# Prompt attention: the shifts of a head turned to rows by one transpose instead of four

## The reference, cut to what matters

```
s_s = einsum(q_r, k_s) * scale ; p_s = masked_softmax(s_s, m_s) ; o_s = p_s @ v_s
s_w = einsum(q_r, k_w) * scale ; p_w = masked_softmax(s_w, m_w) ; o_w = p_w @ v_w
o   = g[0] * o_c + g[1] * o_s + g[2] * o_w        # o_c: the compressed branch
```

## Time and profile before

| | us |
|---|---|
| time, median of 3 runs (1668.59 to 1669.82) | 1668.79 |
| span of the profiled execution, first to last instruction | 1663.0 |
| PE busy, share of the span | 97% |
| DVE busy | 50% |
| ACT busy | 39% |
| POOL busy | 7% |
| q_row copies (L1891), 16 of them, busy in all | 10.9 |
| transposes of the shifts (L1695), 64 of them, busy in all | 10.0 |

### The profile page before, as it was taken

The page is one execution under the profiler, slowest core; times in us unless marked ns, Lnnn a source line. Parts: engine busy times, 40 slices in busy tenths (PEclk is TensorE's granted clock), DMA queues, the critical chain, the costliest instruction groups (busy, mean ns, idle before and its releaser), DMA issues.

```text
span 1663.0 us, 32232 instructions
## 1 busy us (share of the span) xinstructions
PE 1605.1 (97%) x13788; PEld 1472.4 (89%) x13788; DVE 824.2 (50%) x1091; ACT 648.4 (39%) x1141; POOL 117.2 (7%) x146
## 2 busy tenths in 40 slices
PE   8999899999999999999999779999999999999998
PEld 7787699999999999999999545556999999999998
DVE  6988547434343346633343465652473433434372
ACT  5444655323131334521232366665442222323242
POOL 1000000000000000010240352210000000000000
PEclk9999999999999999999999989999999999999999
DMA  7633161332323222322146200002223232322221
GB/s 204 160 93 113 35 206 56 104 98 77 102 77 100 78 82 71 102 83 77 53 135 211 92 1 1 1 14 77 76 77 102 76 102 77 102 77 87 92 77 54
DMA packets 139623, 145.69 MB, mean 88 GB/s; under 512 B 6562, under 2 KB 131314, under 8 KB 139279
## 3 DMA queue, kind: packets, MB, share of 16 engines
q1 hardware_dynamic: 138207, 136.94, 26.2%
q0 software_dynamic: 1280, 6.75, 1.3%
HBM read 130.79 MB, written 10.87 MB: 85 GB/s over the span
## 4 chain that ended last, share of the span: by engine, by line
PE 86%; DVE 7%; ACT 4%; issue 2%; DMA 0%; SPq 0%; DVEq 0%; ACTq 0%
PE ps L389 62%; PE ps L522 2%; PE ps L1215 2%; PE ps L1064 2%; PE ps L1063 2%; PE ps L1065 2%; PE ps L1737 2%; PE ps L1717 2%; DVE w_lo L374 1%; PE ps L1719 1%; PE ps L1664 1%; PE ps L575 1%; ACT w_hi L369 1%; PE ps L1662 1%; DVE resid L688 1%
## 5 line engine op out<-in xcount | busy, mean ns | idle before, releaser
L389 PE MATMUL ps<-x_hi,w_hi 128*128 128x272 f32 x1664 | 360.8, 290 | 11.5 <-DVE x_lo L2530 4.3
L389 PE MATMUL ps<-x_hi,w_lo 128*128 128x272 f32 x1664 | 357.8, 289 | 0.0
L389 PE MATMUL ps<-x_lo,w_hi 128*128 128x272 f32 x1664 | 356.6, 288 | 0.0
L374 DVE TENSOR_TENSOR w_lo<-w_raw,w_hi 128x2048 fp32r<-128x2048 f32 x101 | 233.8, 2315 | 141.4 <-ACT w_hi L369 139.5
L369 ACT ACTIVATE w_hi<-w_raw 128x2048 fp32r<-128x2048 f32 x101 | 192.6, 1907 | 267.6 <-PE ps L389 264.9
L389 PEld LDWEIGHTS ps<-x_hi,w_hi 128*128 128x128 f32 x1664 | 266.9, 189 | 20.5 <-issue 11.5
L389 PE MATMUL ps<-hid_hi,w_hi 128*128 128x272 f32 x1280 | 268.0, 289 | 2.2 <-DVE hid_lo L2038 1.5
L389 PE MATMUL ps<-hid_hi,w_lo 128*128 128x272 f32 x1280 | 267.4, 288 | 0.0
L389 PEld LDWEIGHTS ps<-x_lo,w_hi 128*128 128x128 f32 x1664 | 267.1, 189 | 0.0
L389 PE MATMUL ps<-hid_lo,w_hi 128*128 128x272 f32 x1280 | 266.6, 288 | 0.0
L389 PEld LDWEIGHTS ps<-x_hi,w_lo 128*128 128x128 f32 x1664 | 265.4, 189 | 0.0
(11 more groups left out here) (378 smaller groups left out, 2140.9 us busy)
## 6 DMA issues: line engine op xcount, KB each, us to landing
w_raw<-in_ffn_w_in SPq DMA_DIRECT2D x64, 512.0 KB, 4.5
w_raw<-in_ffn_w_out SPq DMA_DIRECT2D x64, 512.0 KB, 4.3
w_raw<-in_nsa_w_in SPq DMA_DIRECT2D x20, 512.0 KB, 4.5
w_raw<-in_ple_w_gate SPq DMA_DIRECT2D x16, 512.0 KB, 4.3
w_raw<-in_conv_w_in SPq DMA_DIRECT2D x15, 512.0 KB, 5.4
w_raw<-in_conv_w_out SPq DMA_DIRECT2D x8, 512.0 KB, 4.0
w_raw<-in_nsa_w_o SPq DMA_DIRECT2D x8, 512.0 KB, 4.5
conv_in_turned<-conv_in SPq DMA_DIRECT2D x16, 203.2 KB, 2.9
```

The lines of the kernel that those rows point to most:

```text
L374: dve.tensor_tensor(WL[par][:, :], RAW[par][:, :], WH[par][:, :].bitcast(F32), ALU.subtract)\
L389: m = pe.matmul(o_, w[par][:, wcols:wcols + P], x[:, k, c_], start=f, stop=l)
```

## The change

The tile `shift_hi_lo` grows from 32 to 228 columns and is cleared once, by a new memset ahead of L1336. The four shifts of query tile qt now stand at columns 32 qt to 32 qt + 3 of a head's part (the parts of even and odd heads start 128 columns apart; between the groups of four lie zeros). One transpose of 100 columns turns them; query tile qt's four rows come out in PSUM partitions 32 qt to 32 qt + 3, columns 0 to 127. Four copies of 4x128 bring them to where one copy of 4x512 did. The semaphore for the reader rises with the last of the four.

```diff
+        M_W = 3 * 32 + 4 + 4
+
+        def shift_cols(hd):
+
+            x = MROW[:, (hd % 2) * P:(hd % 2) * P + M_W - 4]
+            return x, bass.AP(x.tensor, x.offset, [x.ap[0], [32, QT], [2, 2], [1, 2]])
+
...
-                                               ("shift_hi_lo", [P, 2, QT, 2, 2], F32R), ("soft_cmp", [P, 3, QT, GQ], F32),
+                                               ("shift_hi_lo", [P, P + M_W], F32R), ("soft_cmp", [P, 3, QT, GQ], F32),
...
+            L(dve.memset(MROW[:, :].bitcast(F32), 0.0), wait=False)
             for br in range(2):
                 L(dve.tensor_tensor(SELC[HD:P, br:br + 1], CST[HD:P, C_ID + HD + 2 * br:C_ID + HD + 2 * br + 1],
...
-                for qt in range(QT):
-                    m = pe.transpose(PS[0:4, 7, qt * P:(qt + 1) * P],
-                                     MROW[:, hd % 2, qt, :, :].rearrange("p b h -> p (b h)").bitcast(F32), ID)
-                m.then_inc(S["m_T"], 1)
+                pe.transpose(PS[0:M_W - 4, 7, 0:P], shift_cols(hd)[0].bitcast(F32), ID).then_inc(S["m_T"], 1)
...
-                x, m = hd % 4, MROW[:, hd % 2, :, :, :]
+                x, m = hd % 4, shift_cols(hd)[1]
...
-                L(dve.tensor_copy(QB[c % 3][HD:HD + 4, half, :], PS[0:4, 7, :]), S["m_rows"], wait=False)
+                for qt in range(QT):
+                    L(dve.tensor_copy(QB[c % 3][HD:HD + 4, half, qt * P:(qt + 1) * P], PS[32 * qt:32 * qt + 4, 7, 0:P]),
+                      S["m_rows"] if qt == QT - 1 else None, wait=False)
```

## The result

The changed kernel takes 1675.08 us (median of 21 runs), the kernel before 1668.59 in as many runs of the same chips. The ratio is 1.0042, 95% interval 1.0029 to 1.0054: slower, 0.4% and not the 0.16% of the forecast, and outside its range. The runs of either kernel spread over 8 to 12 us (1661.95 to 1670.37, 1666.87 to 1678.74), far more than the three runs shown before. One slip in the text ahead: the new tile has 232 columns, not 228; its memset took 252 ns.

What follows compares the result with a forecast made beforehand. The prediction took PE (86% of the chain) and DVE (7%) as the bound. Its terms, 0.53 + 0.32 + 3.18 + 0.53 - 0.05 + 0.2 - 1.98 = +2.73 us, on 1668.79 gave 1671.5 us, range 1666.3 to 1673.6.

Steps and rivals of the forecast that it cites:

- an even head: PE at six even heads: one transpose in place of four on the chain saves 0.33 us each, 1.98 in all.
- serial copies: DVE's four copies of a head's rows don't overlap: 1.21 us against 0.68, +0.53; 3.18 over six odd heads.
- The memset: DVE ahead of L1336, on the chain: the larger clear adds +0.2 us, between 0 and 0.3.
- the line on the even heads: Even heads other than 0 and 8: copies end 0.20 us later against PE, DVE has pauses; costed at nothing.
- POOL works hard ahead of the steps: POOL busy 4.7 of 5 us there stretches copies inside SBUF but not the 4x512 copies from PSUM; costed at nothing.
- head 8: Copy on the chain, with a weight split and the maxima behind it on DVE: +0.53 us.
- head 15: Transposes on the chain, copy not: the turned matmul starts slightly earlier, -0.05 us.
- head 0: Ahead of the steps, where DVE is the bound: its longer copies on the chain cost +0.53 us.
- head 1: Ahead of the steps: copy starts 0.21 us earlier after the single transpose, then costs +0.53; net +0.32 us.
- overlapping copies: Rival on DVE's four copies: full overlap gives 1666.4 us, 0.08 us of overlap 1668.3; chance 0.22 together.
- a dear transpose: Rival on PE: the lone transpose costs 0.27 us, saves only 0.17; sum +3.7, 1672.5 us; chance 0.15.
- the clock's fall in the steps: Rival: PE's 1.17 us idle before odd heads' turned matmuls lowers its clock, 2.5 us on top, 1674 us; chance 0.05.

Runs made afterwards that it cites:

- the two-input form: Changed kernel with the compressed branch's minimum as a tensor_tensor against a constant column, not a tensor_scalar: ratio 1.0023, steps 1 to 47 165.41 us.
- the keys in two halves: Changed kernel with DVE doing the first half of a group's keys one step earlier: ratio 1.0037, steps 1 to 47 164.49 us.
- again: The changed kernel once more with no edit, against the kernel before: ratio 1.0028, steps 1 to 47 166.85 us.
- copies first: Changed kernel with the odd heads' copies put ahead of the maxima on DVE: ratio 0.9997, steps 1 to 47 161.61 us.

## Why the prediction was wrong

**Right.** Which heads have their copy on the chain and which their transposes; 0.33 us for an even head (-1.98 forecast, -1.97 measured); serial copies because the input's start moves (1.21 forecast, 1.25 measured; 0.57 a head and not 0.53, 0.24 us over six). The memset: +0.2 forecast, 0.25 measured, plus a gap of 0.03. No clock fell in the steps with PE's pauses of 1.2 us.

**The step that failed** is the line on the even heads: "the copies end 0.53 - 0.33 = 0.20 us later against PE", and DVE has pauses; "nothing". The sign is wrong. At these heads the copies start where the maxima end, so the shorter transpose doesn't bring them forward, while it does bring PE forward: the two add up, 0.53 + 0.33 = 0.86. Measured, behind the start of the turned matmul of step 15 the copies end 0.33 us before the change (1034.09 + 0.68 against 1034.44) and 1.22 after it (1037.90 + 1.25 against 1037.93), 0.89 later. The share of idle time is an average too: behind heads 6 and 10 DVE has no pause, the copies, the keys and the next maxima stand in a row, and what DVE does late there PE pays two steps later: 2 x 0.42 = 0.84 us. By the runs the wrong sign decides it: with the maxima 0.20 and 0.32 us later against PE nothing is lost, with 0.52 it is 0.03, and with 1.00 it is 0.42. Had the 0.20 been true, the "nothing" would have been too. The row for the missing pause was in the trace (the maxima of step 15, at 1037.83 us, began with no idle time in front of them), and I had looked for slack in ACT behind head 6 only the earlier trace rows, where there is some.

**The second** is "POOL works hard ahead of the steps ... I cost that at nothing". It weighed POOL for the copies from PSUM alone, and only ahead of the steps. POOL's memset hangs on PE, and the minimum, behind the late maxima and ACT's logarithm, now starts 0.26 us later against the maxima of step 16: it had just missed the memset and now meets it, 2 x 0.75 us. That the meeting costs this is shown by the two-input form, and that the lateness behind the keys brings it about by the keys in two halves, with which it doesn't happen. The forecast also took head 8 at +0.53 where -0.33 and +0.99 make 0.66, and head 15 at -0.05 where it was +0.08; for these two I have no row that says why.

**The rest.** The steps give +4.66. Ahead of them the memset gives 0.28. From head 0's shift to the first turned matmul the changed kernel took 14.27 to 14.29 us in four profiles (again, keys in halves, minimum in two inputs, copies first), and 15.56 in the first profile, in which the lower clock also lay on the first microseconds behind that shift (964.4 to 967.8 us); the kernel before took 13.9. That is +0.35, where +0.53 for head 0 and +0.32 for head 1 were forecast: head 1's is right, and head 0's came to nothing. A line of the chain of waits and one of POOL's timeline, for the kernel before and, below it, the changed kernel again:

```profile
967.38 0.93 DVE qT L1592
...
967.31 0.95 POOL L1939 MEMSET q_row<- 64x1024 f32 x1
```

```profile
968.23 0.36 DVE qT L1600
...
967.60 0.95 POOL L1946 MEMSET q_row<- 64x1024 f32 x1
```

The first of the eight copies of the samples' result ends 0.05 us behind POOL's memset in both kernels (968.31 against 968.26, 968.59 against 968.55). It takes 0.93 us before and 0.36 now, and head 0's longer copies fill the difference. It is the same oversight as in the second step, POOL costed at nothing, this time in the change's favour and by luck.

Together these are +5.3 us, 0.32%, inside the intervals of both comparisons, where 2.7 was forecast. The second profile of the changed kernel had a span of 1668.3, also 5.3 over the earlier trace rows, but that is luck: ahead of the memset it was 0.9 us early, and its samples' stretch took 1.0 us longer. At an equal clock the runs say +7, so some 2 us more than I can name, outside the steps. It isn't that the changed kernel ran at a lower clock more often: its listed mean is 0.989 over 21 runs and 0.991 over nine, that of the kernel before 0.989 to 0.990 in three sets of 35. A piece of the 2 us may be that the lower clock falls on other work, as in the first profile, where it cost 1.3 us between head 0's shift and the first turned matmul; that is a reading of one profile and not shown.

Of the rivals, overlapping copies and a dear transpose are both refuted, and the clock's fall in the steps did not come.

## What to carry to other kernels

Before a gain on one engine is taken off a loss on another, ask what starts the lengthened instruction: if it isn't the part that got shorter, gain and loss add up. Ask of each engine's queue behind it where its next pause is; a share of idle time says nothing of the one place where three operations stand in a row. When an edit moves one engine against another by some tenths of a us, look at what runs beside POOL: short one-source operations of VectorE in SBUF can grow from 0.17 to 0.89 us by meeting it. And where a consumer waits for a short copy, the order of that copy and the longer work in front of it (0.38 us a head in the steps here) may be worth more than the number of instructions that feed it.

## What the runs showed of the hardware

- Four 4x128 copies from PSUM take 1.25 us if each starts at another 32-partition group of PSUM (0.31 apart), and 0.88 us if all read from one start (0.20 apart), with the same places written.
- A transpose with 100 stationary columns adds 0.12 us to the chain, one with 32 columns 0.11; four in a row of 4 columns each add 0.44.
- A `tensor_scalar` over 16 elements in SBUF took 0.89 and 0.98 us beside a POOL memset, a two-input operation of that size 0.17 beside one and 1.22 beside a POOL operation that reads SBUF.
- With the same instructions, the stretch from 884 us to the first shift took 75.3 us where none of it lay at the lower clock (two profiles), 78.3 with 6.8 us at the lower clock (three), and 79.1 to 79.5 with 10.2 us (nine). Over whole runs 0.001 more of mean clock went with some 1.2 us less.
